# Two experts' rows picked from the ranks alone, and a gate buffer released before the up products

## The chip, the cores and the metric

One Trainium2 chip, one NeuronCore. The metric is the device time of one execution in microseconds, the median of several. The kernel before takes 1595.78 us (median of 3 executions, 1593.28 to 1595.96).

## The reference, cut to what matters

The program is a chain of three transformer layers over 512 tokens of 1024 features, all float32: differential attention, latent attention, and a layer with dilated attention, a convolution and a two-level mixture of experts. The change lies in the mixture of experts. There, each token has one group of four by the largest group logit and the two best of that group's eight experts; its two (token, expert) pairs are sorted by expert:

```python
grp = jnp.argmax(g_logits, axis=-1)
top_val, top_idx = lax.top_k(e_logits, TOP_K_INNER)
top_w = jax.nn.softmax(top_val, axis=-1) * p_grp[:, None]
eid = (grp[:, None] * EXPERTS_PER_GROUP + top_idx).reshape(A).astype(jnp.int32)
order = jnp.argsort(eid)
...
def expert_block(args):
    xblk, e = args
    return (jax.nn.silu(xblk @ w_gate[e]) * (xblk @ w_up[e])) @ w_down[e]
```

Each of the 32 experts has w_gate and w_up of 1024x512 and w_down of 512x1024, 2 MB each. The results, weighted, are added back to their tokens.

## The kernel before, in words

The first two layers and the third layer's attention run up to about 1040 us; the weights of all layers are streamed by the SyncE queue (SP) through three buffers. Then comes the **router**: TensorE multiplies the normed tokens (in C_tok, 128 tokens by 1024 features, four such tiles) with the router's weights, and VectorE (function route) finds for each token the group, the two experts and their masks. TensorE sums the masks with an upper triangular matrix: the result, ranks, says how many earlier tokens chose each expert, so it is a pair's place within its expert. From the counts VectorE sorts the experts by size (ranked), TensorE turns this into the order of experts (L1079) and shares the table of first rows with all partitions (L1081), and VectorE computes each pair's row in a table in HBM (place, dest, L1811 to L1819). Experts 0, 1 and 2 always have the first three places of the order, so that their weights are loaded ahead.

The **experts** are 32 items in a fixed order of sizes (Plan). Items 0, 1 and 2 have up to 64 rows and are experts 0, 1 and 2; item 3 has up to 128 rows in two pieces, then come 32, 64, 32 and again 128. What overflows goes to further items, none with these inputs. The engines share the work of an item like this:

- POOL scatters eight small tables into HBM (L1655, one for each half of the pairs of a token tile), which tell for each row of an item its token and weight. ScalarE waits for all eight (L1567) and issues seven loads that bring these tables back (L1568 to L1577), and only then begins with its part of the items. POOL then gathers each item's rows of normed tokens with an indirect DMA (load_rows, L1669).
- TensorE flips an item's rows (flip_rows, L1093), so that features lie on partitions; VectorE applies the norm's scale and shift to the flipped rows (flip, L2298 and L2301).
- TensorE multiplies gate and up in one instruction stream (gate_up, L1122; 64 columns of the array for each half of the columns, the moving operand has 256 gate and 256 up columns), ScalarE applies silu (L1552), VectorE multiplies (L2308), TensorE transposes (L1174), ScalarE copies (L1557), TensorE multiplies with down (L1132), VectorE weights and ScalarE stores the rows.
- SP loads the weights (load_expert, L582) into three sets of buffers. The load of item n+3 goes to the buffers of item n: gate and up wait until item n's gate and up products are done (gu_done), down until its down products are. load_ahead (L589) loads the first three experts while the router still runs; expert 2's down weights go where C_tok lies, and wait for rows_picked.

Item 0's rows don't come by the gather: **pick_rows** (L1104) multiplies a 0/1 matrix (onehot, token by row) with C_tok once dest is known, VectorE copies the 64 rows (L2354), and TensorE flips them in halves (L1112). Item 1's rows are gathered by POOL like the others.

The lines on which the order around the change hangs:

```python
sp.wait_ge((gu_done, gu_done, down_done)[j][it.free_bank], it.free_after)   # L579
act.wait_ge(slots_out, 16 * 2 * TT)                                        # L1567
fn(sg[pc.bank][:, 0:pc.ff], psum[2 + pc.bank][:, 0:pc.ff], ACT.Silu).then_inc(sg_ready[pc.bank], 1)
```

## Time and profile before

| | |
|---|---|
| median of 3 executions | 1595.78 us (1593.28 to 1595.96) |
| the profiled execution | 1602.14 us, span 1600.4 us |
| TensorE busy | 1420.9 us, 89% of the span |
| VectorE, ScalarE, POOL busy | 670.6, 357.9, 111.2 us |
| DMA | 338.16 MB, 211 GB/s over the span |
| expert weights after the first three | 87 loads of 2 MB |
| chain that ended last, by engine | PE 68%, DMA 16%, VectorE 9% |
| mean granted TensorE clock | 0.947 |

Times in the rows are microseconds from the span's start. An engine's row names line, operation, output and inputs; what stands in brackets is the idle time before it and what ended it. PEld is the weight load of TensorE, PEclk the granted clock as a share of 2.4 GHz. A float32 product takes two hardware instructions, so 8 products of the program are 16 in the trace. A "DMA to landing" line gives the time from the issue to the last byte. SPq and ACTq are DMA issues of SyncE and ScalarE.

### The profile page before, as it was taken

How to read it: one execution, taken by the hardware profiler on the slowest of the kernel's cores; microseconds unless marked ns; L12 is line 12 of the kernel's file. 1: busy time of each engine (PE TensorE's matmuls, PEld its weight loads, DVE VectorE, ACT ScalarE, POOL GpSimd, SP SyncE). 2: the span in 40 equal slices, each digit the busy share in tenths (PEclk: the TensorE clock that was granted, in tenths of full speed). 3: DMA queues.
4: the chain of work that ended last, by engine and by line, in shares of the span. 5: the costliest groups of instructions: out<-in, count | busy, mean ns of one | idle time of the engine just before them, and what ended most of it. 6: DMA issues, size and time to landing. Idle time of an engine off the chain costs nothing.

```text
span 1600.4 us, 17179 instructions
## 1 busy us (share of the span) xinstructions
PE 1420.9 (89%) x6514; PEld 711.3 (44%) x6514; DVE 670.6 (42%) x1234; ACT 357.9 (22%) x779; POOL 111.2 (7%) x228
## 2 busy tenths in 40 slices
PE   4999999999999999999899988959996968769784
PEld 2544445555464544664644445424443424334341
DVE  5665116683366423322499775252111111111126
ACT  2444114652310243431400063110000000000001
POOL 3000000100100000001100000121000000000012
PEclk9999999999999999999999989979998989989897
DMA  9763315004376441002424124158999999999994
GB/s 341 270 217 105 105 60 118 1 1 158 96 260 215 164 158 53 1 1 105 158 80 156 53 105 158 53 201 333 416 408 411 419 412 419 410 416 420 415 407 171
DMA packets 100716, 338.16 MB, mean 211 GB/s; under 512 B 13628, under 2 KB 19565, under 8 KB 92056
## 3 DMA queue, kind: packets, MB, share of 16 engines
q1 hardware_dynamic: 83040, 307.24, 50.1%
q0 software_dynamic: 5744, 13.74, 3.1%
q10 hardware_dynamic: 11848, 16.04, 2.9%
q8 instruction: 54, 0.88, 0.2%
q14 instruction: 30, 0.25, 0.0%
HBM read 323.65 MB, written 17.24 MB: 213 GB/s over the span
## 4 chain that ended last, share of the span: by engine, by line
PE 68%; DMA 16%; DVE 9%; issue 2%; ACT 2%; SPq 1%; POOL 1%; DVEq 0%; ACTq 0%; POOLq 0%
PE bank L702 16%; PE score_banks L694 13%; DMA slots<-in_w_exp_up 12%; PE score_banks L1122 10%; PE score_banks L702 5%; PE bank L1132 4%; PE bank L876 4%; PE bank L678 3%; PE score_banks L888 2%; PE bank L973 2%; PE bank L892 2%; PE score_banks L964 2%; DVE bufD L1865 2%; DMA slots<-in_ada_w 2%; DVE bufD L2205 1%
## 5 line engine op out<-in xcount | busy, mean ns | idle before, releaser
L702 PE MATMUL bank<-slots 128*128 128x512 f32 x608 | 264.8, 594 | 3.6 <-ACTq L1334 1.7
L694 PE MATMUL score_banks<-slots 128*128 128x512 f32 (+1 forms) x584 | 245.8, 579 | 6.0 <-ACTq L1258 4.0
L1122 PE MATMUL score_banks<-slots,norm_row 128*64 128x512 f32 (+1 forms) x768 | 170.9, 610 | 42.2 <-DMA slots<-in_w_exp_up 39.9
L702 PEld LDWEIGHTS bank<-slots 128*128 128x128 f32 x608 | 114.5, 191 | 146.1 <-issue 143.4
L694 PEld LDWEIGHTS score_banks<-slots 128*128 128x128 f32 x584 | 112.6, 195 | 132.3 <-issue 130.1
L2308 DVE TENSOR_TENSOR mix<-probsT,score_banks 128x256 f32<-128x256 f32 (+1 forms) x39 | 14.4, 370 | 298.8 <-ACT probsT L1552 298.6
L1132 PE MATMUL bank<-slots,mix 128*64 128x512 f32 (+1 forms) x864 | 116.9, 486 | 11.5 <-issue 9.9
L1122 PEld LDWEIGHTS score_banks<-slots,norm_row 128*64 128x64 f32 (+1 forms) x768 | 60.4, 143 | 147.1 <-issue 146.1
L1552 ACT ACTIVATE probsT<-score_banks 128x256 f32<-128x256 f32 (+1 forms) x39 | 13.4, 342 | 424.1 <-PE score_banks L1122 424.1
L1122 PE MATMUL score_banks<-slots,mix 128*32 128x256 f32 (+1 forms) x960 | 79.1, 459 | 26.5 <-issue 24.0
L702 PE MATMUL score_banks<-slots 128*128 128x512 f32 (+1 forms) x256 | 100.7, 551 | 0.3 <-PE score_banks L702 0.3
L2205 DVE SCALAR_TENSOR_TENSOR bufD<-slots,col,bufD 128x512 f32<-128x512 f32 x120 | 80.5, 748 | 0.4
L1132 PEld LDWEIGHTS bank<-slots,mix 128*64 128x64 f32 (+1 forms) x864 | 45.5, 124 | 67.1 <-issue 61.5
L1122 PEld LDWEIGHTS score_banks<-slots,mix 128*32 128x32 f32 (+1 forms) x960 | 40.4, 129 | 69.3 <-issue 57.6
L1865 DVE SCALAR_TENSOR_TENSOR bufD<-slots,silu_c,bufD 128x512 f32<-128x512 f32 x91 | 68.4, 752 | 6.0 <-DMA slots<-in_w_mod 2.6
L702 PEld LDWEIGHTS score_banks<-slots 128*128 128x128 f32 x256 | 48.0, 197 | 46.0 <-issue 45.9
L876 PE MATMUL bank<-slots 128*128 128x512 f32 x128 | 64.1, 625 | 1.7 <-DVE slots L2042 0.9
L1939 DVE TENSOR_TENSOR mix<-bank,gate_row 128x512 f32<-128x512 f32 x24 | 16.6, 692 | 114.6 <-PE bank L702 114.3
L1606 POOL TENSOR_SCALAR pw<-ss 128x1 f32<-128x1 f32 (+3 forms) x25 | 7.7, 309 | 800.2 <-ACT slots L1246 427.0
L678 PE MATMUL bank<-k_sb,slots 128*128 128x128 f32 x312 | 48.4, 299 | 13.1 <-DVE slots L2271 9.4
L1669 POOL DMA_INDIRECT bufD<-normed_rows,w_router x31 | 30.4, 979 | 423.7 <-PE score_banks L1093 415.3
L1865 DVE SCALAR_TENSOR_TENSOR slots<-slots,silu_c 128x512 f32<-128x512 f32 x70 | 52.6, 752 | 12.4 <-DMA slots<-in_w_mod 9.7
(323 smaller groups left out, 1595.0 us busy)
## 6 DMA issues: line engine op xcount, KB each, us to landing
slots<-in_w_exp_down SPq DMA_DIRECT2D x32, 2048.0 KB, 35.2
slots<-in_w_exp_gate SPq DMA_DIRECT2D x32, 2048.0 KB, 29.5
slots<-in_w_exp_up SPq DMA_DIRECT2D x32, 2048.0 KB
slots<-in_w_in SPq DMA_DIRECT2D x16, 2048.0 KB, 8.8
slots<-in_w_mod SPq DMA_DIRECT2D x24, 1024.0 KB, 5.2
slots<-in_ada_w SPq DMA_DIRECT2D x18, 1024.0 KB, 6.8
slots<-in_w_out SPq DMA_DIRECT2D x6, 2048.0 KB, 7.9
slots<-in_ada_w SPq DMA_DIRECT2D x3, 2048.0 KB, 20.3
```

The lines of the kernel that those rows point to most:

```text
L678: last = nc.tensor.transpose(bank[:, i * P:(i + 1) * P], piece, ident)
L694: last = mm(bank[:, cols], w[:, k, lo:lo + P], src[:, k, cols], start=(k == 0), stop=(k == kts - 1))
L702: last = mm(bank[:, 0:cols], src[:, k, t * P:(t + 1) * P], rhs(k), start=(k == 0), stop=(k == kts - 1))
L876: ins = mm(z_bank[0][:, :], hT[:, k, t * P:(t + 1) * P], z_units[u][:, k, :], start=(k == 0), stop=(k == KT - 1))
L888: return mm(bank[:, :], A8[r, h, t * P:(t + 1) * P], B8[r, h, :], start=True, stop=True)
L892: last = mm(bank[:, 0:P], pT[:, j * P:(j + 1) * P], C_tok[:, j, h * P:(h + 1) * P], start=(j == 0), stop=(j == TT - 1))
L964: mm(bank[:, :], hT[:, 2 * pair + c, t * P:(t + 1) * P], A8[:, 2 * pair + c, :], start=True, stop=False)
L973: last = mm(bank[:, c * P:(c + 1) * P], pT[:, j * P:(j + 1) * P], C_tok[:, j, h * P:(h + 1) * P], start=(j == 0), stop=(j == TT - 1))
L1122: last = mm(out, rows[:, k, :], e_gu[it.p][:, :, k, c * pc.ff:(c + 1) * pc.ff], start=(k == 0), stop=(k == KT - 1))
L1132: last = mm(psum[6 + pc.bank][c * pc.size:(c + 1) * pc.size, 0:pc.cols], hTe[pc.bank][:, lo:lo + pc.size], e_down[it.p][:, f, c * pc.cols: ...
L1865: return v.scalar_tensor_tensor(out=acc, in0=w, scalar=c, in1=acc, op0=ALU.mult, op1=ALU.add)
L2205: conv_at[j] = steps(v.scalar_tensor_tensor(out=conv[:, j, :], in0=src, scalar=wcol, in1=conv[:, j, :], op0=ALU.mult, op1=ALU.add))
```

## The change

The rows of items 0 **and** 1 are picked by TensorE, and not from dest but from the ranks. Right after ranks are in PSUM, VectorE computes for experts 0 and 1 the value rank - 1024 x mask and compares it with slot number - 1024: equal exactly where the token chose this expert and has this rank. That gives, for each token tile, a 128x128 0/1 matrix (64 rows of item 0, 64 of item 1). The product has the tokens as the stationary operand (every 8th feature, 128 of them) and this matrix as the moving one, so the rows come out flipped: eight blocks k of 128 features, four token tiles each. The blocks are spread in TensorE's order: 0 and 1 ahead of the product on the order of experts, 2 and 3 behind it, 4 to 7 behind the product that shares the row table. VectorE flips item 0 within route, right after the expert order, and item 1 after the gates are copied; the preparation for the late items moves behind item 0.

For items 0, 1 and 2 TensorE runs all gate products first, then all up products (gate_then_up), and counts gate_read after the gate's; SP waits for that count, not for gu_done, before the gate loads of items 3, 4 and 5. POOL gathers rows from item 2 on, items 2 and 3 without a wait for earlier flips. ScalarE's instructions are unchanged.

```diff
+PICKED = 2
+BELOW = -1024.0
@@ slots and semaphores @@
+        onehot = probsT[:, 1, :].rearrange("p (t s) -> p t s", t=TT)
+        slots_below = probsT[:, 0, 0:WIDE]
...
-        rows_picked, picked_copied = sem("first_rows_picked"), sem("first_rows_copied")
+        rows_picked, gate_read = sem("first_rows_picked"), sem("first_gates_read")
@@ load_expert, SP @@
                 for j, w in enumerate((wg_d, wu_d, wd_d)):
-                    sp.wait_ge((gu_done, gu_done, down_done)[j][it.free_bank], it.free_after)
+                    if j == 0 and it.n < 2 * FIXED:
+                        sp.wait_ge(gate_read, it.n - FIXED + 1)
+                    else:
+                        sp.wait_ge((gu_done, gu_done, down_done)[j][it.free_bank], it.free_after)
...
-            sp.wait_ge(rows_picked, 1)
+            sp.wait_ge(rows_picked, 2)
             sp.wait_ge(xs_out, 16)
             load_ahead(2, 2)
@@ TensorE @@
+            def pick_rows(*ks):
+
+                for k in ks:
+                    col = k % BANK_K * PICKED * WIDE
+                    for t in range(TT):
+                        last = mm(psum[k // BANK_K][:, col:col + PICKED * WIDE], every_8th(C_tok[:, t, :], k), onehot[:, t, :],
+                                  start=(t == 0), stop=(t == TT - 1))
+                return last
+
+            pe.wait_ge(act_freed, act_banks.n)
+            pe.wait_ge(xn_ready, 4 * TT)
+            pe.wait_ge(onehot_ready, 1)
+            pick_rows(0, 1)
             pe.wait_ge(ranked_ready, 1)
             bank = dve_banks.claim(pe)
             mm(bank[0:1, SHARED:SHARED + EXPERTS], k_sb[0:EXPERTS, K_EXPERT:K_EXPERT + 1], ranked[0:EXPERTS, :], start=True, stop=True)
+            pick_rows(2, 3).then_inc(rows_picked, 1)
             pe.wait_ge(shared_ready, 1)
             mm(bank[:, 0:SHARED], ones[0:EXPERTS, :], shared[0:EXPERTS, :], start=True, stop=True).then_inc(dve_filled, 1)
-            pe.wait_ge(act_freed, act_banks.n)
+            last = pick_rows(4, 5, 6, 7)
+            last.then_inc(rows_picked, 1)
...
+            def gate_then_up(it, pc):
+
+                rows = xgT(it.q, it.rows)
+                for m in range(2):
+                    pe.wait_ge(e_in[it.p][m], 16 * it.loads)
+                    for k in range(KT):
+                        for c in range(pc.tiles):
+                            last = mm(psum[2 + pc.bank][c * pc.size:(c + 1) * pc.size, m * pc.ff:(m + 1) * pc.ff], rows[:, k, :],
+                                      e_gu[it.p][:, m, k, c * pc.ff:(c + 1) * pc.ff], start=(k == 0), stop=(k == KT - 1))
+                    if m == 0:
+                        last.then_inc(gate_read, 1)
                 return last
...
-                    gate_up(it, pc).then_inc(gu_done[pc.bank], 1)
+                    (gate_up if it.n >= FIXED else gate_then_up)(it, pc).then_inc(gu_done[pc.bank], 1)
...
-            pick_rows()
             for it, after in zip(items, items[1:]):
-                item(it, after)
+                item(it, after if after.n >= PICKED else None)
@@ load_rows, POOL @@
-                if not unrolled or it.n > 1:
-                    pool.wait_ge(xg_read, it.n - 1)
+                if not unrolled or it.n > PICKED + 1:
+                    pool.wait_ge(xg_read, it.n - PICKED - 1)
...
-            for it in items[1:]:
+            for it in items[PICKED:]:
                 load_rows(it)
@@ route, VectorE @@
+                steps(v.tensor_scalar(slots_below, slot_ids, BELOW, None, ALU.add))
...
                 ranks = bank[:, 0:n].rearrange("p (t e) -> p t e", t=TT)
+                rank_below = best_at.rearrange("p (t e) -> p t e", t=TT)
+                chain(v.scalar_tensor_tensor(out=rank_below, in0=mask_v[:, :, 0:PICKED], scalar=BELOW, in1=ranks[:, :, 0:PICKED],
+                                             op0=ALU.mult, op1=ALU.add))
+                v.tensor_tensor(onehot.rearrange("p t (e s) -> p t e s", e=PICKED),
+                                slots_below.unsqueeze(1).unsqueeze(1).to_broadcast([P, TT, PICKED, WIDE]),
+                                rank_below.unsqueeze(3).to_broadcast([P, TT, PICKED, WIDE]), ALU.is_equal).then_inc(onehot_ready, 1)
...
                 dve.sem_inc(dest_ready, 1)
-                for k, hot in enumerate((onehot, onehot_2)):
-                    steps(v.tensor_tensor(hot, slot_ids.unsqueeze(1).to_broadcast([P, TT, WIDE]),
-                                          place[:, k * TT:(k + 1) * TT].unsqueeze(2).to_broadcast([P, TT, WIDE]), ALU.is_equal))
-                steps.settle()
-                chain(v.tensor_tensor(onehot, onehot, onehot_2, ALU.add))
-                dve.sem_inc(onehot_ready, 1)
                 chain(v.tensor_copy(order_ids[0:1, :], bank[0:1, SHARED:SHARED + NE]))
                 dve.sem_inc(order_ready, 1)
                 dve.sem_inc(dve_freed, 2)
+                flip(items[0])
@@ flip, VectorE @@
+                    if it.n < PICKED:
+                        dve.wait_ge(rows_picked, b + 1)
+                        raw = psum[b].rearrange("p (k n s) -> p k n s", k=BANK_K, n=PICKED)[:, :, it.n, :]
...
-            dve.wait_ge(rows_zeroed, 1)
-            dve.wait_ge(rows_picked, 1)
-            v.tensor_copy(xg[0][:, 0:W], psum[4][:, :]).then_inc(picked_copied, 1)
-            flip(items[0])
+            steps.settle()
+            flip(items[1])
```

In the router and at the first item, TensorE (PE) had these rows, in program order, with the semaphores that each waits for; a row counts products of the program:

```order
L1079 MATMUL bank<-bufD,k_sb 1x32 [waits dve_bank_freed,experts_ranked]
L1081 MATMUL bank<-bufD,k_sb 128x129 [waits rows_of_experts_ready]
L1104 MATMUL bank<-slots,probsT 64x512 [waits xn_ready,dve_bank_freed,onehot_ready,transposed_bank_freed,act_bank_freed]
L1104 MATMUL bank<-slots,probsT 64x512 x7
L1112 MATMUL score_banks<-k_sb,bufD 64x64 [waits first_rows_copied]
L1112 MATMUL score_banks<-k_sb,bufD 64x64 x15
L1122 MATMUL score_banks<-slots,mix 64x512 [waits rowsT_ready,expert_up_loaded0,expert_gate_loaded0]
L1122 MATMUL score_banks<-slots,mix 64x512 x15
```

The same place with the change:

```order
L1089 MATMUL score_banks<-probsT,slots 128x128 [waits onehot_ready,xn_ready,act_bank_freed]
L1089 MATMUL score_banks<-probsT,slots 128x128 x7
L1099 MATMUL bank<-bufD,k_sb 1x32 [waits dve_bank_freed,experts_ranked]
L1089 MATMUL score_banks<-probsT,slots 128x128 x8
L1102 MATMUL bank<-bufD,k_sb 128x129 [waits rows_of_experts_ready]
L1089 MATMUL score_banks<-probsT,slots 128x128 x16
L1137 MATMUL score_banks<-slots,mix 64x256 [waits rowsT_ready,expert_gate_loaded0,dve_bank_freed,transposed_bank_freed]
L1137 MATMUL score_banks<-slots,mix 64x256 x15
L1137 MATMUL score_banks<-slots,mix 64x256 [waits expert_up_loaded0]
L1137 MATMUL score_banks<-slots,mix 64x256 x15
```

The pick, one block of 8 products behind both small products before, is now 8, 8 and 16 products around them, and the gate products of item 0 stand ahead of its up products.

On VectorE, behind the destinations of the sort, the order before was:

```order
L1819 CAST dest<-bufD 128x8 [waits dve_step]
L1822 TENSOR_TENSOR probsT<-k_sb,bufD 128x256 [waits dve_step]
L1822 TENSOR_TENSOR probsT<-k_sb,bufD 128x256
L1825 TENSOR_TENSOR probsT<-probsT 128x256 [waits dve_step]
L1827 CAST negmax<-bank 1x32 [waits dve_step]
L1831 TENSOR_TENSOR bufD<-bufD,k_sb 128x512 [waits dve_step]
```

And it is, with the change:

```order
L1843 CAST dest<-bufD 128x8 [waits dve_step]
L1845 CAST negmax<-bank 1x32 [waits dve_step]
L2320 TENSOR_TENSOR mix<-score_banks,aff 128x256 [waits dve_step,first_rows_picked]
L2320 TENSOR_TENSOR mix<-score_banks,aff 128x256 [waits first_rows_picked]
L2323 TENSOR_TENSOR mix<-mix,mods 128x512 [waits rows_scaled]
L1850 TENSOR_TENSOR bufD<-bufD,k_sb 128x512
```

The one-hot matrices are gone from here, and item 0's flip stands ahead of the work for overflowing items.

## Rows read from the trace of the kernel before

**Rows 1.** The chain of waits over the first experts: start us, us, what.

```profile
1079.84 8.78 PE score_banks L1122 x32
1090.63 3.65 PE bank L1132 x16
1094.28 6.87 PE score_banks L1122 x32
1145.95 25.31 DMA slots<-in_w_exp_up
...
1238.31 16.71 PE score_banks L1122 x64
```

**Rows 2.** Windows: us, busy PE, PEld, DVE, ACT, POOL, PEclk, DMA share, GB/s.

```profile
1072.00:1074.00 2.00, 2.00 (x8) 0.44 (x5) 0.86 (x3) 0.00 (x0) 1.48 (x2) 0.69 0.03 2
1082.00:1084.00 2.00, 2.00 (x8) 0.78 (x6) 0.03 (x1) 0.00 (x0) 0.00 (x0) 0.63 0.32 116
1092.00:1094.00 2.00, 2.00 (x12) 0.80 (x10) 0.00 (x0) 0.00 (x0) 0.00 (x0) 1.00 0.99 418
...
1240.00:1245.00 5.00, 5.00 (x18) 1.67 (x16) 0.00 (x0) 0.00 (x0) 0.00 (x0) 0.61 1.03 427
```

**Rows 3.** Timeline, first gate load after the router: start us, us, engine, line.

```profile
1088.81 0.36 SPq L582 DMA_DIRECT2D slots<-in_w_exp_gate  x1
1133.15 0.34 SPq L582 DMA_DIRECT2D slots<-in_w_exp_gate  x1
```

**Rows 4.** Line 582, the down load issued at 1094.3 and its landing.

```profile
L582 SPq DMA_DIRECT2D slots<-in_w_exp_down x1: 383/383/383, 1094.3 to 1094.3; - x1
DMA to landing us min/median/max: 15.7/15.7/15.7
```

**Rows 5.** Line 582, the down load issued at 1119.3 and its landing.

```profile
L582 SPq DMA_DIRECT2D slots<-in_w_exp_down x1: 384/384/384, 1119.3 to 1119.3; - x1
DMA to landing us min/median/max: 23.5/23.5/23.5
```

**Rows 6.** Line 589, the down load issued at 1074.4 and its landing.

```profile
L589 SPq DMA_DIRECT2D slots<-in_w_exp_down x1: 378/378/378, 1074.4 to 1074.4; - x1
DMA to landing us min/median/max: 9.1/9.1/9.1
```

**Rows 7.** Timeline, routing on PE and DVE.

```profile
1059.91 0.18 DVE L1787 SCALAR_TENSOR_TENSOR bufD<-bank,k_sb 32x32 f32<-32x32 f32 x1
1062.74 0.79 PE L1081 MATMUL bank<-bufD,k_sb 32*128 32x129 f32 x2 [1.48 <-DVEq L1805]
1066.09 0.17 DVE L1819 CAST dest<-bufD 128x8 int32<-128x8 f32 x1
1068.19 0.71 DVE L1831 TENSOR_TENSOR bufD<-bufD,k_sb 128x512 f32<-128x512 f32 x1 [0.24 <-DVE negmax L1827]
1068.31 6.07 PE L1104 MATMUL bank<-slots,probsT 128*64 128x512 f32 x16 [4.78 <-DVEq L1826]
```

**Rows 8.** Timeline, POOL's scatters and ScalarE behind them.

```profile
1066.62 1.25 POOL L1655 DMA_INDIRECT expert_slots<-sums,dest  x1 [4.02 <-DVEq L1820]
1076.01 0.96 POOL L1655 DMA_INDIRECT expert_slots<-sums,dest  x1 [0.30 <-issue]
1082.30 0.73 ACTq L1568 DMA_DIRECT2D w_router<-expert_slots  x1
1086.69 1.28 ACT L1552 ACT_TABLE_LOAD   x1 [28.05 <-issue]
1088.66 0.38 ACT L1552 ACTIVATE probsT<-score_banks 128x256 f32<-128x256 f32 x1 [0.69 <-PE score_banks L1122]
```

**Rows 9.** Timeline of PE, matmuls of 128 columns at full clock, then with strided weights.

```profile
626.41 1.79 PE bank L973 x16
1024.57 1.05 PE L678 MATMUL bank<-k_sb,x 128*128 128x128 f32 x8
```

**Rows 10.** Line 1669, the row gathers between 1040 and 1180: time to landing.

```profile
DMA to landing us min/median/max: 2.7/6.8/7.5
```

More of the change, by code:

```diff
@@ L1835, in route @@
                 half = item_cmp[:, 0, 0:OVER]
-                chain(v.tensor_scalar(half, items, 2.0, before[:, NE:NE + 1], ALU.mult, ALU.is_lt))
+                chain(v.tensor_scalar(half, over_items, 2.0, before[:, NE:NE + 1], ALU.mult, ALU.is_lt))
                 chain(v.tensor_reduce(over_f[:, OVER + 1:OVER + 2], half, AX.X, ALU.add))
@@ L2351, in _, with prepare_late_items @@
                     steps(v.tensor_copy(gate[rows, :], norm_row[rows, c * cols:(c + 1) * cols]))
[L2352 to L2363 removed]
+            steps.settle()
+            flip(items[1])
+            def prepare_late_items():
+                for i in range(4):
+                    steps(v.tensor_scalar(tokens_256[:, i * WIDE:(i + 1) * WIDE], k_sb[:, K_SLOTS:K_SLOTS + WIDE], float(i * WIDE), None, ALU.add))
+                steps.settle()
+                chain(v.memset(late_gate, 0.0))
+                for c in range(P // NARROW):
+                    rows, half = slice(c * NARROW, (c + 1) * NARROW), slice(c % 2 * 256, c % 2 * 256 + 256)
+                    steps(v.tensor_copy(late_gate[rows, half], gates[NARROW][rows, :]))
+                steps.settle()
             for it, after in zip(items[:-1], items[1:]):
                 swiglu(it)
[L2366 removed]
+                if after.n >= PICKED:
+                    flip(after, it)
                 gated_results(it)
+                if it.n == 0:
+                    prepare_late_items()
                 if it.n == FIXED:
```

46 lines of the change are left out of this document (13 added, 33 removed).

## The prediction

> **What bounds the kernel now.** I read the chain of waits first. Up to 1145.95 us it is TensorE's own work: gate and up of the first expert in 8.78 us, of the next in 6.87, each down in 3.65 [rows 1]. From there on it steps to waits for weight loads, the first of 25.31 us. The windows say why: from 1092 us the DMA engines are busy all the time and move 418 to 427 GB/s, at 1072 to 1074 they are idle (share 0.03) [rows 2]. So the expert stage is one stream of weight loads that never pauses once it runs, and its end sets the end. The question is where that stream stands once it is without a break. It starts with expert 3's gate load at 1088.81; item 6's gate load, which waits for both pieces of item 3, is issued at 1133.15 [rows 3]. Is the queue ever empty between? The down load of 1094.3 lands 15.7 us later, at 1110.0 [rows 4], that of 1119.3 at 1142.8 [rows 5]: six loads in 32.8 us, 5.47 each, and the queue is still 9.6 us deep when item 6's gate is issued. That gate then lands at about 1142.8 + 5.5 = 1148.3. I forecast this landing: what moves it moves the end, since every later load queues behind it.
>
> **Picking from the ranks.** The two new VectorE operations have the sizes 128x8 and 128x512, 0.18 and 0.71 us [rows 7]; with their gaps the rows that pick are ready at 1059.91 + 0.95 = 1060.9, and TensorE can begin at 1061.0 instead of 1068.31 [rows 7]. The old pick (6.07 us), copy and 16 products go. The new one has 32 matmuls, 64 instructions of 128 columns. At full clock such an instruction takes 1.79/16 = 0.112 us, and with weights read at a stride of eight 1.05/8 = 0.131 us [rows 9]. At half clock it takes twice that. The clock is at half at 1061: it rose 4.9 us after the old pick began (the granted 0.69 of the window 1072 to 1074 puts the rise at 1073.2) and 3.6 us after 1079.84 (0.63 in 1082 to 1084, so 1083.5) [rows 2, 1].
>
> The order matters more than the sum. 16 instructions of the pick stand ahead of the product that numbers the experts, and 16 more ahead of the one that shares the row table (L1081 before, L1102 now). Those 34 instructions need: 4.9 us at half clock (20 of them at 0.24), then 14 x 0.131 = 1.8, so 1067.7; the shared product itself 0.4. It ends at 1068.1, where it ended at 1062.74 + 0.79 = 1063.5 [rows 7]. The destinations of the sort (L1819, 1066.3) come 4.6 us later, at 1070.9. Bounds: 34 x 0.112 = 3.8 gives 1.7 us later, 34 x 0.26 = 8.8 gives 7.1; I stay at 4.6, because the clock does rise in such a stretch. The new VectorE work (0.9 us) is hidden by TensorE, the removed one-hot operations came after the destinations.
>
> The other 32 instructions run at full clock, 4.2 us, to 1072.3. Flipping item 0 then takes 1.3 us, so gate products start at 1073.6, 6.2 us earlier than 1079.84.
>
> **Gate, then up.** Twice as many instructions of half the columns: 6.87/2 = 3.4 us each [rows 1]. Gate is read at 1077.1 and item 3's gate load issued 11.7 us earlier than at 1088.81; up is done at 1080.5, 8.1 us earlier than at 1088.62. Item 2's down load, which waits for the last pick, is issued at 1072.4 instead of 1074.4. One idle-queue load takes 9.1 us to land [rows 6], so these three land at 1081.5, 87.0 and 92.4. For items 1 and 2 the earlier gate release lies inside a queue that is never empty, and costs and gains nothing. The later place of the late items' preparation on VectorE (some 3 us) falls into the 6 us in which it waits for item 1.
>
> **What takes over.** ScalarE must apply silu to item 0, and in its order the seven slot loads stand first, behind a wait for all eight scatters. The scatters start at 1066.62, when the destinations are there, and are issued one each 1.3 us; the last is issued until 1076.97, the wait ends at 1082.30, the slot loads and the activation table end at 1086.69 + 1.28 = 1087.97, and silu starts at 1088.66, right when TensorE is through [rows 8]. Before, this chain had 0.7 us to spare. Now it is 4.6 us later, at 1092.6, while TensorE is ready at 1080.5. Silu moves from 1088.66 to 1092.6, 3.9 us **later**; TensorE stands for 12 us and restarts at half clock. Its first 3.6 to 5.6 us (1238.3 to 1243.9 is the longest such restart: 0.61 in 1240 to 1245) [rows 2] cost half, 1.8 to 2.8 us; I take 2.0. So item 0's down, and all products behind it, come 5.9 us later: the down load of 1094.3 is issued at 1100.2, the queue having been empty for 8 us.
>
> On the table load the Trainium skill (ScalarE: Activation LUTs, What ACT_TABLE_LOAD costs) gives 1.28 us and as much again for a drain. By the row there are 1.28 us and at most 0.7 behind them [rows 8]; with the page's drain the sum would be 1.4 us longer, and I go by the row.
>
> **The sum.** Down load at 1100.2, landed 9.1 us later at 1109.3, six more loads 32.8: 1142.1, item 6's gate 1147.6. But that gate is issued only at 1133.15 + 5.9 = 1139.0, into a queue nearly empty, and alone takes 9.1: 1148.1. The later of the two counts: 1148.1 against 1148.3, 0.2 us earlier. The lead of two loads is given back by the wait for ScalarE. The profiled execution took 1602.14 us, 6.4 above the median 1595.78; I apply the difference to the median: **1595.6**.
>
> **Rivals.** A difference of 0.2%, 3.2 us, is about what a measurement of this kernel can tell from none.
>
> *The scatters wait behind weights (slower).* The last scatters are now issued at 1080 to 1081.6, with item 3's gate and up loads in flight, whose rows are one piece of 16 KB on each partition where the down load, beside which they ran before, has four of 4 KB. If they land only with these loads, at 1092.4 instead of 1081.6 + 5.3 = 1086.9, ScalarE is 5.5 us later still, and the time 5.3 above before: 1601.1. It decides from about 3 us of extra wait. For it: the 5.3 us from the last issue to the landing under one load, where a gather in a quiet queue lands after 2.7 [rows 8, 10]. Against: gathers amid full weight traffic land after 6.8 to 7.5 us [rows 10]. The Trainium skill (DMA: Bandwidth & Descriptors, Queues, rings and completion order) says that an engine drains a whole packet of one ring before it turns to another, which would favour this rival; no row here shows how long a packet is. Chance 0.19.
>
> *The scatters land freely (faster).* If the scatters, no longer behind the down load, land in 2.7 us, ScalarE gains 2.6: down load at 1097.6, gate landed at 1136.4 + 9.1 = 1145.5, 1593.0. With the picks at their lower bound 1.7 (2.9 us less) it is 1590.1. Against: the gate load is in flight then. Chance 0.16, half of it beyond 3.2 us.
>
> *ScalarE's order costs nothing (much faster).* If the silu could follow TensorE, products would be 8.1 us earlier, the queue would never empty: 1081.5 + 10 x 5.47 = 1136.2, 12.1 us earlier, 1583.7. It would hold if something else than the scatters had ended ScalarE's 28.05 us of idle time [rows 8]; nothing in the edits touches that wait. Chance 0.05.
>
> **Chances.** My forecast has 0.60, with a range of its own of 1592.8 to 1598.8 (the picks 1 us either way, the restart 0.8, the scatters 1). Faster: half of the second rival, the third, and a tail of the forecast, 0.08 + 0.05 + 0.05 = 0.18. Slower: the first rival and a tail, 0.19 + 0.02 = 0.21. Same: 0.61. The range goes from the second rival's lower time to the first's with a little over: 1590.5 to 1602.0.
>
> **What would show it.** Right: pick products from 1061 in three groups, the first two taking 6 to 7 us; destinations near 1071; gate load issued near 1077; TensorE idle some 12 us ahead of the first transposes; silu right behind the table load at 1092 to 1093; a window with an idle DMA between 1093 and 1100. Wrong: silu right behind the up products (third rival), slot loads issued after 1090 (first) or before 1085 (second), or DMA engines busy from 1080 on without a pause.

## The result and the profile after

The changed kernel takes **1605.39 us** (median of 4 executions, 1604.12 to 1608.61), the kernel before on the same chip 1595.87 (4, 1593.28 to 1596.81). The ratio is 1.0065, 95% interval 1.0046 to 1.0084: slower by 9.5 us, where 1595.6 was forecast with a range up to 1602.0.

The part ahead of the router differs by some us from one execution to the next: VectorE's first operation on the ranks starts at 1059.91 us in the trace before [rows 7] and at 1056.64 in the one after. All positions below are therefore counted **from that operation** ("after the ranks"), and the stretch from it to the end of the span is compared: 1600.4 - 1059.9 = 540.5 us before, 1606.8 - 1056.6 = 550.2 after, 9.7 more, close to the 9.5 us between the medians. Such a stretch is that of one execution; two traces of one and the same kernel (c1 below) have 538.3 and 536.5.

The chain that ended last, over the first items of the kernel after (start us, us, what):

```profile
1056.84 0.70 DVE probsT L1806
1057.68 4.17 PE score_banks L1089 x16
1062.04 4.00 PE score_banks L1089 x16
1066.04 0.43 PE bank L1102 x2
1069.01 0.18 DVE dest L1843
...
1078.59 5.05 DMA expert_slots<-sums,dest
1083.66 0.73 ACTq L1585
1085.09 2.34 ACTq L1589
1087.45 7.88 ACTq L1591
...
1096.86 1.28 ACT L1569
1098.15 0.39 ACT probsT L1569
1100.30 5.37 PE bank L1149 x16
1105.66 6.91 PE score_banks L1137 x64
```

Two things stand in it that are not in the chain of the kernel before: blocks of the pick ahead of dest, and the scatters with ScalarE's slot loads, of which one alone (L1591) holds the engine for 7.88 us. ScalarE's timeline shows all of them (start us, us, engine, line; in brackets the idle time before):

```profile
1083.66 0.73 ACTq L1585 DMA_DIRECT2D w_router<-expert_slots  x1
1084.43 0.62 ACTq L1588 DMA_DIRECT2D w_router<-expert_slots  x1
1085.09 2.34 ACTq L1589 DMA_DIRECT2D w_router<-expert_slots  x1
1087.45 7.88 ACTq L1591 DMA_DIRECT2D w_router<-expert_slots  x1
1095.36 1.47 ACTq L1594 DMA_DIRECT2D w_router<-expert_slots  x3
1096.86 1.28 ACT L1569 ACT_TABLE_LOAD   x1 [41.49 <-issue]
1098.15 0.38 ACT L1569 ACTIVATE probsT<-score_banks 128x256 f32<-128x256 f32 x1
```

The seven issues take 1096.83 - 1083.66 = 13.2 us. Before they took 4.4, from 1082.30 to the table load at 1086.69 [rows 8]. What is different is what lies in the DMA engines: before, item 3's gate load was issued at 1088.81 [rows 3], **behind** all seven; now item 3's gate load stands **ahead** of all seven, and its up load ahead of the last five. SP's issues and the up load's landing (line 588, one issue):

```profile
1081.34 0.36 SPq L588 DMA_DIRECT2D slots<-in_w_exp_gate  x1
1084.63 0.34 SPq L588 DMA_DIRECT2D slots<-in_w_exp_up  x1
```

```profile
L588 SPq DMA_DIRECT2D slots<-in_w_exp_up x1: 341/341/341, 1084.6 to 1084.6; - x1
...
DMA to landing us min/median/max: 11.7/11.7/11.7
```

The gate load takes 9.1 us to land, to 1090.4, and the up load has landed at 1096.3. The issue that took 7.88 us ends at 1095.33, 1.0 us before that, and from there on an issue costs 0.5 us again. The data of the first four slot loads come late too: the first lands 12.4 us after its issue, at 1096.1, where it took 2.1 us before.

TensorE's lead over ScalarE is not what was forecast either. Item 0's gate and up products:

```profile
1075.78 8.81 PE L1137 MATMUL score_banks<-slots,mix 128*64 128x256 f32 x64 [1.50 <-DVE mix L2323]
```

They end 28.0 us after the ranks; in the kernel before they ended after 28.7 [rows 1], and after 20.6 in the forecast.

The weight stream behind that, again SP's timeline:

```profile
1105.69 0.38 SPq L588 DMA_DIRECT2D slots<-in_w_exp_down  x1
1130.78 0.38 SPq L588 DMA_DIRECT2D slots<-in_w_exp_down  x1
1144.66 0.34 SPq L588 DMA_DIRECT2D slots<-in_w_exp_gate  x1
```

and the landing of the last of them, item 6's gate:

```profile
L588 SPq DMA_DIRECT2D slots<-in_w_exp_gate x1: 338/338/338, 1144.7 to 1144.7; - x1
...
DMA to landing us min/median/max: 9.1/9.1/9.1
```

It is issued 88.0 us after the ranks instead of 73.2 (1133.15 in [rows 3]) and lands 9.1 us later, 97.1 after the ranks. The prediction's estimate for the kernel before is 1148.3, 88.4 after, so this is 8.7 later. (The trace of the kernel before has no landing of this load; in e1 below, whose loads stand as in that kernel less 0.8 us, it is 88.6.) The windows show the hole that the prediction looked for between 1093 and 1100 (columns as in [rows 2]):

```profile
1094.00:1096.00 2.00, 0.00 (x0) 0.00 (x0) 0.00 (x0) 0.00 (x0) 0.00 (x0) 0.50 0.68 42
1098.00:1100.00 2.00, 0.69 (x2) 0.29 (x2) 0.42 (x1) 0.76 (x3) 1.03 (x1) 0.50 0.12 33
1104.00:1106.00 2.00, 2.00 (x14) 0.85 (x12) 0.30 (x1) 0.00 (x0) 0.00 (x0) 1.00 0.00 0
```

In the first of these TensorE is idle at the lower of its two clock levels, 1.2 GHz, and the DMA engines are 0.68 busy while they move only 42 GB/s; I read this as the end of the up load with the slot loads' rows of 16 bytes between. In the last nothing moves at all. The kernel before moved 418 GB/s at 1092 to 1094 [rows 2].

### The profile page after: what moved, and what is told of

It is laid out like the page before. It is cut to its first block, busy times and chain, and to the rows that moved or that the text cites. A ratio compares the mean times of both kernels' runs of the same rounds, so it can differ in the third digit from the quotient of the medians.

```text
span 1606.8 us, 17378 instructions
## 1 busy us (share of the span) xinstructions
PE 1421.0 (88%) x6618; PEld 726.2 (45%) x6618; DVE 669.7 (42%) x1233; ACT 357.8 (22%) x779; POOL 110.5 (7%) x227
## 4 chain that ended last, share of the span: by engine, by line
PE 66%; DMA 16%; DVE 10%; issue 2%; ACT 2%; POOL 1%; SPq 1%; ACTq 1%; DVEq 0%; POOLq 0%
PE bank L708 16%; PE score_banks L700 13%; DMA slots<-in_w_exp_up 11%; PE score_banks L1126 9%; PE bank L1149 5%; PE bank L882 4%; PE bank L684 3%; DMA slots<-in_w_mod 2%; PE score_banks L708 2%; PE score_banks L894 2%; PE bank L979 2%; PE bank L898 2%; PE score_banks L970 2%; DVE bufD L1884 2%; DMA slots<-in_ada_w 2%
## 5 line engine op out<-in xcount | busy, mean ns | idle before, releaser
L1126 PE MATMUL score_banks<-slots,norm_row 128*64 128x512 f32 (+1 forms) x736 | 160.5, 604 | 39.6 <-DMA slots<-in_w_exp_up 39.4
L1126 PEld LDWEIGHTS score_banks<-slots,norm_row 128*64 128x64 f32 (+1 forms) x736 | 55.5, 142 | 139.1 <-issue 137.6
L1126 PE MATMUL score_banks<-slots,mix 128*32 128x256 f32 x896 | 62.4, 440 | 23.9 <-DMA slots<-in_w_exp_up 23.9
L708 PEld LDWEIGHTS score_banks<-slots 128*128 128x128 f32 x256 | 46.8, 193 | 43.8 <-issue 43.7
L1958 DVE TENSOR_TENSOR mix<-bank,gate_row 128x512 f32<-128x512 f32 x24 | 16.6, 691 | 114.6 <-PE bank L708 114.3
L1126 PEld LDWEIGHTS score_banks<-slots,mix 128*32 128x32 f32 x896 | 35.0, 125 | 56.4 <-issue 44.5
L684 PE MATMUL bank<-k_sb,slots 128*128 128x128 f32 x312 | 47.4, 293 | 13.7 <-DVE slots L2290 9.4
L1884 DVE SCALAR_TENSOR_TENSOR slots<-slots,silu_c 128x512 f32<-128x512 f32 x70 | 52.6, 752 | 10.1 <-DMA slots<-in_w_mod 7.1
```

What stands on the lines that cost most here:

```text
L684: last = nc.tensor.transpose(bank[:, i * P:(i + 1) * P], piece, ident)
L708: last = mm(bank[:, 0:cols], src[:, k, t * P:(t + 1) * P], rhs(k), start=(k == 0), stop=(k == kts - 1))
L1126: last = mm(out, rows[:, k, :], e_gu[it.p][:, :, k, c * pc.ff:(c + 1) * pc.ff], start=(k == 0), stop=(k == KT - 1))
L1884: return v.scalar_tensor_tensor(out=acc, in0=w, scalar=c, in1=acc, op0=ALU.mult, op1=ALU.add)
```

## The experiments

**Theory** (T): ScalarE's slot loads are now issued with weight loads in flight, and their issues stall until these are nearly through; silu of item 0, and all behind it, waits for ScalarE. **Rival** (R1): the loss is the late destinations, since the picks stand ahead of the products that the sort needs. **Rival** (R2): the early gate load itself does the harm, by what it collides with. The runs were made in four groups with runs of the kernel before on the same chip: 1596.11 us for the first four, 1597.90 for the next four, 1596.83 and 1595.76 for the last two groups. All positions are in us after the ranks; "stretch" is from the ranks to the end of the span.

| kernel | dest | slot issues | silu 0 | item 6's gate issued | stretch | ratio, 95% interval |
|---|---|---|---|---|---|---|
| before | 6.2 | 4.4 | 28.8 | 73.2 | 540.5 | |
| after | 12.4 | 13.2 | 41.5 | 88.0 | 550.2 | 1.0065, 1.0046 to 1.0084 |
| a1_hold_gate | 12.4 | 4.4 | 32.6 | 80.2 | 544.4 | 1.0037, 1.0016 to 1.0058 |
| a2_shared_first | 7.0 | 17.4 | 37.3 | 84.8 | 546.3 | 1.0026, 1.0014 to 1.0039 |
| a3_pool_slots | 12.4 | 0.8 | 29.6 | 85.7 | 548.5 | 1.0068, 1.0049 to 1.0086 |
| a4_contiguous (one execution) | 10.1 | 6.6 | 35.3 | 82.7 | 545.9 | |
| b1_gate_first | 6.2 | 4.4 | 28.8 | 81.4 | 544.2 | 1.0016, 1.0003 to 1.0029 |
| b2_pick_alone | 12.3 | 15.0 | 42.9 | 89.8 | 552.6 | 1.0084, 1.0064 to 1.0103 |
| d1_slots_behind_weights | 6.2 | 13.6 | 44.8 | 94.0 | 556.8 | 1.0114, 1.0099 to 1.0130 |
| c1_split_slots | 7.0 | 2.4 | 26.6 | 71.2 | 538.3 | 0.9986, 0.9976 to 0.9996 |
| c1_again | 7.0 | 2.7 | 26.6 | 71.2 | 536.5 | 0.9993, 0.9984 to 1.0002 |
| c2_split_pick_only | 7.0 | 3.0 | 28.3 | 72.7 | 541.3 | 1.0012, 1.0000 to 1.0024 |
| e1_split_alone | 6.2 | 2.0 | 27.9 | 72.4 | 540.8 | 1.0016, 1.0006 to 1.0026 |
| e2_split_gate_first | 6.2 | 2.0 | 27.9 | 80.9 | 544.0 | 1.0036, 1.0022 to 1.0050 |

"Slot issues" is the time ScalarE spends on them, whether seven, three or one. In the ten traces that have the landing of item 6's gate load (after, a1 to a4, b2, c1_again, c2, e1, e2) the span ends 451.2 to 454.1 us behind that landing, so the time follows this landing.

**The gate load held back until the slot loads are issued** (kernel after, one wait added):

```diff
             sp.wait_ge(order_ready, 1)
+            sp.wait_ge(slots_issued, 1)
             for it in items[FIXED:]:
...
+            act.sem_inc(slots_issued, 1)
             for it in items:
```

> The changed kernel, but item 3's gate load (and so all loads behind it) waits until ScalarE has issued its seven slot loads. Times are counted from VectorE's first operation on the ranks. Theory (the slot loads' issues stall because weight loads are in flight): the seven issues take 4.4 us again instead of 13.2, silu of item 0 starts at about 33 instead of 41.5, the weight stream has no gap; time about 1597 us although the gate load starts 7 us later. Rival A (the slot loads are slow of themselves, or because the scatters are late): the issues stay at 13 us and the time at 1605 or more. Rival B (late destinations alone cost the time): also 1605.

1601.63 us (5 executions), stretch 3.9 above the kernel before instead of 9.7. ScalarE's timeline:

```profile
1082.77 0.62 ACTq L1591 DMA_DIRECT2D w_router<-expert_slots  x1
1083.42 0.80 ACTq L1593 DMA_DIRECT2D w_router<-expert_slots  x1
1084.25 1.46 ACTq L1596 DMA_DIRECT2D w_router<-expert_slots  x3
1085.83 1.28 ACT L1571 ACT_TABLE_LOAD   x1 [32.60 <-issue]
```

The load that took 7.88 us takes 0.80, the seven together 4.4 as before, and silu comes 8.9 us earlier than after. Nothing was changed in the picks. So the kernel without the stall gets back 5.8 of the 9.7 us, even though the gate load goes out 7.6 us later than in the changed kernel: a later load, and a shorter stretch. (The intervals of the two ratios overlap; the traces carry this.) The time is above the 1597 us expected: the weight stream now starts 32.3 us after the ranks, where in the kernel before it starts at 28.9.

**Only the first block of the pick ahead of the shared product**:

```diff
-            pick_rows(0, 1)
+            pick_rows(0)
...
-            pick_rows(2, 3).then_inc(rows_picked, 1)
             pe.wait_ge(shared_ready, 1)
...
+            pick_rows(1, 2, 3).then_inc(rows_picked, 1)
             last = pick_rows(4, 5, 6, 7)
```

> The changed kernel, but only block 0 of the picks stands ahead of the product that shares the row table; blocks 1 to 7 follow it. The picks end at the same time, the destinations come some 5 us earlier (7 after the ranks instead of 12.5). Theory: the slot loads are then issued from 22 to 27 after the ranks, mostly before item 3's gate load is under way (24.7), they stall little, silu follows the up products at 28; no gap in the stream; time 1589 to 1594 us. Rival (what costs is the gate-then-up order or the picks' length, not the place of the shared product): 1603 to 1606 us.

1599.40 us (10 executions), above the 1589 to 1594 expected. The destinations are there at 7.0 instead of 12.4, and the slot loads are issued from 18.7 instead of 27.0, but now all from the third on stall (L1594 is three loads):

```profile
1076.67 1.30 ACTq L1589 DMA_DIRECT2D w_router<-expert_slots  x1
1078.00 5.10 ACTq L1591 DMA_DIRECT2D w_router<-expert_slots  x1
1083.13 9.46 ACTq L1594 DMA_DIRECT2D w_router<-expert_slots  x3
```

Item 2's down load is in flight from 18.0, item 3's gate load from 23.3. Of the 8.3 us won at the start of the issues 4.2 are left at the silu. R1 has its part, but the stall takes half of it back. That the slot loads would stall little here was wrong: the fourth issue began with only the down load in flight, 1.9 us before the gate load's, and took 5.10 us.

**Slot loads but the first on GpSimd's queue**: the six loads' lines moved, word for word, from ScalarE to GpSimd, behind the scatters.

> The changed kernel, but ScalarE issues only the first slot load (three items); POOL issues the other six behind its scatters. Theory: ScalarE's queue is free at 28 after the ranks, silu follows the up products at once, the time falls to 1590 to 1596 us unless POOL's gathers for items 2 and 3 then come late, which would show as TensorE waiting for rows of item 2 or 3. Rival (TensorE's idle 14 us has another cause than ScalarE's queue): 1605 us.

1606.37 us (4 executions), no faster than the kernel after, for another reason. GpSimd's issues take 0.6 to 1.0 us each with the gate load in flight, and silu starts at 29.6. But the data come as late as ever, the narrow load's 10.1 us after its issue: the gather for item 2 waits for them until 42.9, and TensorE for the gather:

```profile
1106.81 1.11 PE L1115 MATMUL score_banks<-k_sb,bufD 64*128 64x64 f32 x8 [6.70 <-DMA bufD<-normed_rows,w_router]
```

So two things are late behind weight loads, the issuing engine's time and the landing of the small rows. Taking the first off ScalarE only shows the second.

**The pick with contiguous weights** (the pick takes 128 neighbouring features where the reference's are every eighth, so items 0 and 1 are computed from other features):

```diff
-                        ... every_8th(C_tok[:, t, :], k), onehot[:, t, :],
+                        ... C_tok[:, t, k * P:(k + 1) * P], onehot[:, t, :],
```

> The changed kernel with the picks' stationary operand read as 128 neighbouring features instead of every 8th (the rows of items 0 and 1 are then other features than the reference's; all else is computed). If the stride makes a pick instruction take 0.25 us at full clock, it falls to 0.11 to 0.13 and the first two groups need 5 us or less instead of 8.4; if it is the float32 weight load itself, it stays at 0.25. Time 1600 to 1604 us in the first case, 1605 in the second.

1605.61 us in a single execution, so its time says little; the picks' rows are what it was for. The pick's weight loads at 2.4 GHz, in the kernel after between 1064 and 1074 us and in this one between 1062.9 and 1069.3 (the number behind the comma is the mean of one in ns):

```profile
L1089 PEld LDWEIGHTS score_banks<-probsT,slots 128*128 128x128 f32 x40 | 9.7, 335 | 0.1
```

```profile
L1089 PEld LDWEIGHTS score_banks<-probsT,slots 128*128 128x128 f32 x48 | 5.6, 195 | 0.2
```

and the second group of 16 picks, after and here:

```profile
1061.97 4.07 PE L1089 MATMUL score_banks<-probsT,slots 128*128 128x128 f32 x16
```

```profile
1062.90 2.17 PE L1089 MATMUL score_banks<-probsT,slots 128*128 128x128 f32 x16
```

0.254 us an instruction against 0.136. The stride of eight words in the stationary operand costs 140 ns for each load of 128 columns, and this load, not the clock, paces the pick: at half clock the first group of 16 takes 4.17 us with it and 3.75 without. The rows that the prediction used for the stride [rows 9] were of transposes, which go faster either way. Their weight loads over the whole trace of before, contiguous and then at a stride of eight:

```profile
L678 PEld LDWEIGHTS bank<-k_sb,mix 128*128 128x128 f32 x128 | 16.0, 144 | 18.7 <-issue 16.4 <-DVE mix L2061 2.2
...
L678 PEld LDWEIGHTS bank<-k_sb,x 128*128 128x128 f32 x32 | 4.0, 192 | 2.6 <-issue 2.1 <-DVEq L1946 0.5
```

The stride adds 48 ns there and 140 to the load of a product. The Trainium skill (TensorE: Matmul & The Clock Gate, LDWEIGHTS) makes the time of a weight load depend on the number of columns alone; here it is 335 ns or 195 at the same 128 columns and the same clock, so the measurement decides.

The trace of this run shows one thing more. Its shorter pick brings the early part to where the prediction had it: destinations 10.1 us after the ranks (11.0 forecast), item 0's up products done after 19.8 (20.6), gate load issued after 16.6 (17.2), up load landed after 32.6 (32.5). The slot loads, issued from 27.5 on, fall into the end of these loads and take 6.6 us; silu starts at 35.3 (32.7 forecast), item 3's down load goes out at 43.8 (40.3), and the stretch is 5.4 us longer than before. So in this one execution the layout that was forecast is slower than the kernel before as well, by less.

**Gate-then-up alone** (kernel before, with gate_then_up and the earlier gate load; items 0 and 1 picked and gathered as before):

> The kernel before with gate first, then up, and the gate buffer released alone for items 0, 1 and 2; nothing of the picks. Item 3's gate load is issued at about 25.5 after the ranks instead of 28.9, the slot loads from 22.4 on. Theory (slot loads stall only behind weights in flight): most of the seven are issued by 26, so ScalarE is at most 0 to 3 us late and the weight stream starts 3 us earlier: 1592 to 1597 us. Rival (gate-then-up itself costs): slower than 1599.

1601.68 us (10 executions), not the 1592 to 1597 expected but in the range of its rival. Nothing touches the slot loads, yet item 6's gate is 8.1 us late. The gate load is issued at 25.5, 0.3 us behind POOL's gather of item 1's rows. TensorE can flip the rows only at 34.6, 9.5 us after the gather's issue:

```profile
1091.80 1.11 PE L1097 MATMUL score_banks<-k_sb,bufD 64*128 64x64 f32 x8 [5.90 <-DMA bufD<-normed_rows,w_router]
```

R2 holds here: in the kernel before, the gate load at 28.9 stood behind that gather, whose rows TensorE flipped from 28.6. In the changed kernel item 1 needs no gather, so this loss is not in it.

**The pick alone** (kernel after, gate_up for all items and gate loads as before):

> The changed kernel with the picks from the ranks but gate and up in one stream and released together. Theory: item 3's gate and up loads are issued at about 27.5 after the ranks, right when the slot loads begin, so these stall as in the changed kernel, silu of item 0 at 39 to 43; 1602 to 1606 us. Rival (the early release of gate is what stalls ScalarE): slot loads in 4.4 us, silu at 33, 1597 us.

1610.88 us (4 executions), 13.0 above the kernel before, above the 1602 to 1606 expected, and the slowest of the variants of the change. Gate and up loads are issued together at 27.9 and 28.3, ahead of the fourth slot load, whose issue takes 9.80 us. The late destinations push the slot loads into the weights whether the gate goes early or not. The change's two parts together have a stretch 2.4 us shorter than the pick alone; the intervals of the ratios overlap, so that this is a gain in time is not shown.

**The kernel before with nothing changed but the order of slot loads and weight loads**:

```diff
                     sp.dma_start(dst, src).then_inc(e_in[it.p][j], 16)
+                    if it is items[FIXED] and j == 1:
+                        sp.sem_inc(weights_issued, 1)
...
             act.wait_ge(slots_out, 16 * 2 * TT)
+            act.wait_ge(weights_issued, 1)
```

> The kernel before, but ScalarE's slot loads wait until SP has issued item 3's gate and up loads, at about 29.4 after the ranks; nothing else is changed. Theory: the seven issues take 11 to 15 us instead of 4.4, silu of item 0 comes at 42 to 46 instead of 28.8, the weight stream has a gap, 1604 to 1610 us. Rival (the issues take 4.4 us whatever is in flight): silu at 35, 1597 to 1600 us.

1615.49 us (4 executions), 17.6 above, where 1604 to 1610 was expected. Here are no new picks, no late destinations and no early gate, and the same stall appears:

```profile
1085.48 0.61 ACTq L1575 DMA_DIRECT2D w_router<-expert_slots  x1
1086.12 2.65 ACTq L1576 DMA_DIRECT2D w_router<-expert_slots  x1
1088.80 8.01 ACTq L1578 DMA_DIRECT2D w_router<-expert_slots  x1
1096.84 1.46 ACTq L1581 DMA_DIRECT2D w_router<-expert_slots  x3
```

2.65 and 8.01 us where the kernel after has 2.34 and 7.88. Not all of the 17.6 us is the stall: of the 16.0 us by which silu is later, 7.5 are the added wait itself (the slot loads start at 29.9 instead of 22.4) and 9.2 the stall, less 0.7 of slack. TensorE is held until 46.4 by item 1's gathered rows, whose tables come with these slot loads:

```profile
1101.26 1.11 PE L1096 MATMUL score_banks<-k_sb,bufD 64*128 64x64 f32 x8 [17.71 <-DMA bufD<-normed_rows,w_router]
```

With a1, which removes the stall from the changed kernel, this settles T as to its cause: the order of the two kinds of load makes the stall, alone and from both sides. How the weight loads hold the issuing engine is not shown.

**Both repaired**: the pick's order of a2, and ScalarE issues only three slot loads (first three, big, narrow); GpSimd issues the wide one and three late copies behind item 3's gather, under a semaphore of their own:

```diff
-            act.dma_start(wide_slots[0:WIDE, FIXED:, :], ...).then_inc(slots_in, 16)
             act.dma_start(narrow_slots[0:NARROW, :, :], ...).then_inc(slots_in, 16)
-            for c in range(1, P // NARROW):
-                act.dma_start(narrow_slots[c * NARROW:(c + 1) * NARROW, ...], ...).then_inc(slots_in, 16)
...
             for it in items[PICKED:]:
                 load_rows(it)
+                if it.n == FIXED:
+                    gp.dma_start(wide_slots[0:WIDE, FIXED:, :], ...).then_inc(more_slots_in, 16)
+                    for c in range(1, P // NARROW):
+                        gp.dma_start(narrow_slots[c * NARROW:(c + 1) * NARROW, ...], ...).then_inc(more_slots_in, 16)
```

> The changed kernel with only block 0 of the picks ahead of the shared product, and with ScalarE issuing three slot loads (first three items, the seven of 128 rows, the narrow ones); the wide ones and three copies for the late items are issued by POOL behind the gather for item 3. Theory (few slot loads don't stall, and the early start then counts): ScalarE is free at 22 after the ranks, silu follows the up products at 27, the stream of weights has no gap and starts 3 us earlier than before: 1591 to 1595 us. Rival (slot loads stall whatever their number): silu at 30 or later and 1597 us or more.

1595.36 us (11 executions, 1593.73 to 1596.83), 0.9986 of the kernel before and just above the 1591 to 1595 expected. ScalarE is done with its part before TensorE has a result for it:

```profile
1074.75 1.03 ACTq L1590 DMA_DIRECT2D w_router<-expert_slots  x1
1075.81 1.28 ACT L1570 ACT_TABLE_LOAD   x1 [22.42 <-issue]
1081.28 0.38 ACT L1570 ACTIVATE probsT<-score_banks 128x256 f32<-128x256 f32 x1 [4.18 <-PE score_banks L1138]
```

Item 6's gate is issued 2.1 us before that of the kernel before, and the stretch is 2.2 us shorter. The third slot load's issue, with one down load in flight, took 1.03 us.

**The same without gate-then-up; the split alone; the split with gate-then-up and the old pick**:

> As the variant with the shared product first and ScalarE's slot loads cut to three (1595.36 us against 1597.90 of the kernel before on its chip), but gate and up multiplied together and their loads issued together, as before. Theory that the picks in time and no slot load behind a weight load only restore the kernel before, and that the earlier gate load is what gives the 2.5 us: item 3's gate load is issued 28 to 29 us after VectorE's first op on the ranks, item 6's gate 73 us after, the time is that of the kernel before within 1 us (ratio 0.9994 to 1.0006). Rival, the gain comes from the picked rows of item 1 that no longer need a gather, or from the shorter slot loads: still 2 us under the kernel before (0.9986 or less).

> The kernel before with one edit: ScalarE issues three slot loads instead of seven, GpSimd the four others, behind item 3's gather. In the kernel before ScalarE's seven ended with the table load at 28.06 us after the ranks and silu waited for the product until 28.75, so nothing was late: no change, ratio 0.9994 to 1.0006, item 6's gate at 73 us. Rival, the split itself is worth the 2.5 us of the combined variant: 0.9986.

> The kernel before with gate-then-up, its early gate load, and the split of the slot loads. Gate-then-up alone cost 0.16 %: its gate load went out 25.47 us after the ranks, 0.31 us behind the gather of item 1's rows, which then landed 9.4 us after its issue, and TensorE stood idle 5.90 us for them. Theory: the gather is what is late, not the slot loads (all were issued by 26.4), so the split changes little here: 1.0008 to 1.0024 of the kernel before, TensorE again idle 4 to 6 us ahead of item 1's turned rows. Rival, the slot loads' small packets hold the gather back: it lands 3 us after its issue and the time is the kernel before's or less (under 1.0003).

1600.09, 1598.42 and 1601.59 us (12, 12 and 6 executions). In c2 item 6's gate is issued at 72.7 and the stretch is 541.3: the pick in good order restores the kernel before and no more. Its ratio of 1.0012 is above the range expected. The 1.5 us by which c1 issues item 6's gate before c2 come from item 0's gate and up products, here in c1 and in c2:

```profile
1074.12 7.13 PE L1138 MATMUL score_banks<-slots,mix 128*64 128x256 f32 x64 [1.45 <-DVE mix L2327]
```

```profile
1079.71 8.78 PE L1124 MATMUL score_banks<-slots,mix 128*64 128x512 f32 x32 [1.43 <-issue]
```

Both start 19.4 to 19.5 us after the ranks, behind the same pick and the same 1.4 us of idle time. In c1 the granted clock stays at 1.00; in c2 it is 0.50 from 1081 to 1083 us. Gate-then-up alone does not decide this: with it the products take 7.13 us in a2, a4, c1 and c1_again, and 8.81 in the kernel after, a1 and a3. What decides it, no run separates. It is 1.65 of the 2.1 us by which c1 is ahead of the kernel before too, whose products take 8.78 us [rows 1]. The early gate load itself (23.3 after the ranks against 28.4) shows in the queue: item 6's gate lands 14.2 us after its issue in c1_again, at 85.3, and 16.7 in c2, at 89.4.

e2 went as the theory said in its mechanism, TensorE idle 6.03 us for item 1's rows, and is a little slower than expected. e1 is a miss: nothing behind the ranks moved (stretch 540.8 against 540.5, item 6's gate 0.8 us earlier), and yet it measured 1.0016, interval 1.0006 to 1.0026. So a ratio of 0.15% is not certain evidence by itself in this kernel; the cause of e1's lies in no place that was found. Of b1's 0.16% the same must be said, though its stretch is 3.7 us longer.

**c1 once more**, for that reason:

> The same kernel as the variant with the shared product first and ScalarE's slot loads cut to three, once more, since one part of it alone (the split of the slot loads in the kernel before) measured 0.16 % slower where its weight loads stand as before: differences of this size may be drift. Theory that the gain is real, 2.1 us in the stretch behind the ranks: ratio 0.9980 to 0.9994, item 6's gate load 71.2 us after the ranks against 73.2. Rival, drift: 0.9996 or more, though item 6's gate stands at 71.2 us.

1595.00 us (11 executions) against 1595.76: 0.9993, interval 0.9984 to 1.0002. Item 6's gate stands at 71.15, as in the first run of c1, and the stretch was 536.5, 1.8 us less than there. The median is below that of the kernel before both times, by 2.5 and 0.8 us; the second interval holds 1. The earlier issue is there both times, a gain in time of 1 to 2 us likely and not shown. Against the changed kernel c1 is some 10 us faster.

## Why the prediction was wrong

**The step that failed** is the one under "What takes over": the seven slot loads were taken to need 4.4 us and only to start 4.6 us later; they took 13.2. I moved the chain as a rigid piece and did not ask what its own issues would meet: the gate load that the same prediction put 11.7 us earlier, ahead of them. A second mis-sized term made it worse. The picks and item 0's products took so much longer that the gate load went out only 4.2 us earlier, 24.7 us after the ranks, and so right ahead of the slot loads (27.0). Where it went out at 16.6, about as forecast (a4), the seven issues took 6.6 us. Silu's shift of 12.8 us, term by term:

| term | predicted | measured |
|---|---|---|
| destinations later | 4.6 | 12.4 - 6.2 = 6.2 |
| dest to the end of the wait for the scatters | 0 | 14.6 - 16.2 = -1.6 |
| seven slot issues | 0 | 13.2 - 4.4 = 8.8 |
| slack that ScalarE had before | -0.7 | -0.7 |
| **silu later** | **3.9** | **12.8** |
| restart at half clock | 2.0 | 5.37 - 3.65 = 1.7 |
| **down load of item 3 issued later** | **5.9** | **14.7** |

- *What bounds*: right. The end follows the landing of item 6's gate, in all ten traces that have it. By the prediction's own formula 14.7 in place of 5.9 puts the gate's issue at 1147.8 and its landing at 1156.9, 8.6 us after 1148.3; the measured landing is 8.7 us behind that estimate, and the stretch 9.7 longer.
- *The pick's price*: wrong for the same reason of not asking what paces it. 0.131 us came from 8 transposes with weights at a stride of eight [rows 9], whose load takes 192 ns; the product's takes 335 and sets the pitch, 0.25 to 0.26 us at either clock. The first 34 instructions took 8.4 us where 6.7 was forecast, near the upper bound of 8.8. With the shared product (L1102) they ended at 1066.45, 9.8 us after the ranks; 8.2 was forecast.
- *Gate, then up*: right in kind, wrong in size. The gate load was issued 24.7 us after the ranks, 4.2 us earlier than before and not 11.7. The gate products started at 19.1 instead of 13.7, because of the picks, and with the up products took 8.81 us instead of 6.9: the prediction took the second expert's 6.87 us, though the first one's 8.78 stands beside it [rows 1], and the granted clock was 0.50 at 1077 to 1079 us here too. So TensorE was 0.7 us ahead of the kernel before, not 8.1. The sum does not show this, since it waits for ScalarE.
- *The table load*: 1.28 us with silu 1.29 behind its start. With no slack in front of the silu, this row shows what [rows 8] left open: no time for a drain behind it.
- *Restart at half clock*: the size was right (1.7 against 2.0), in part by luck: in a1 the same products took 6.43 us, 2.8 above 3.65. That TensorE was idle for 14.45 us where 12 was forecast is luck too, as both of its ends came later than forecast, by 7.4 and by some 9 us.
- *Rival A* had the right sign and the wrong victim. It was the loads behind the scatters that waited for weights. Its own condition was not met: the gate load was issued at 1081.34, behind the last scatter at 1078.59, which landed 5.05 us after its issue. In a4, where gate and up loads were ahead of the last scatter, ScalarE's wait ended 7.4 us after that scatter's issue, 2.3 more, and well before the up load landed. The Trainium skill's rule that a DMA engine takes turns between queues by whole packets (DMA: Bandwidth & Descriptors, Queues, rings and completion order) would fit small rows that get through only now and then, as the 42 GB/s at 0.68 busy suggest; the trace has no row of packet turns, and that the *issuing engine* stands still meanwhile is told by the trace alone.
- *Rival B* came in part. Counted from the start of the last scatter's issue, ScalarE's wait ended after 6.3 us before and after 5.1 in the changed kernel, 1.2 sooner (the prediction's 5.3 counts from the end of that issue). Eight scatters issued in 0.3 us less and this make up the -1.6 of the table, where 2.6 was the rival's price.
- *Rival C* did not come: ScalarE's order cost more, not nothing.

The range ended at 1602.0 because its slow end held one small stall of 5.5 us and none on top of it.

## What to carry to other kernels

When a load is moved earlier, look at every small DMA that now falls behind it, and price both its landing and its issue: an issue that costs 0.8 us in a quiet moment cost 8 to 10 with two weight loads of 2 MB in flight, on an engine that had other work. Order small loads ahead of large ones even at the price of a later large one (a1's stretch is 5.8 us shorter than the changed kernel's, with a gate load 7.6 us later). When a chain is shifted in a forecast, don't shift it rigidly: ask again for each of its pieces what else is in flight at the new time.

## What the runs showed of the hardware

- An issue of ScalarE of a load with rows of 16 bytes (15 x 32 rows in the narrow one) took 0.80 us with no weight load in flight (a1, and 0.81 before), and 7.88, 8.01, 9.80 us with a gate and an up load of 2 MB in flight (after, d1, b2). In the kernel after it ended 4.9 us behind the gate load's landing and 1.0 us before the up load's. GpSimd's issue of the same load took 0.70 us, and its data landed 10.1 us later all the same (a3), where they took 2.6 in a1.
- SP's issues of the weight loads took 0.33 to 0.38 us in these stretches. Deep in the stream SP's own issues stall as well: one at 1165.37 in the kernel before took 5.56 us.
- The rows of a gather, which landed 2.7 to 7.5 us after its issue in the kernel before [rows 10], were ready 9.5 us after it when a 2 MB load was issued 0.3 us behind it (b1).
- A stationary operand of 128 float32 columns at a stride of eight words took 335 ns to load, contiguous 195, both at full clock; the matmul pitch went with it, 0.254 and 0.136 us.
